# Summing sixteen of the 24 adaLN weight blocks on VectorE, one layer of a hybrid diffusion backbone on Trainium2

## What is computed

```
mod = silu(cond) @ w_ada + b_ada      # cond 2 x 2048, w_ada 2048 x 12288
shift1, scale1, gate1, shift2, scale2, gate2 = split(mod, 6)
h = rms_norm(x) * (1 + scale1) + shift1
m = mixer(h)        # Hyena branch and attention branch, from one projection w_in, gated, then w_out
x = x + gate1 * rms_norm(m)
h = rms_norm(x) * (1 + scale2) + shift2
x = x + gate2 * rms_norm(experts(h))   # 16 SwiGLU experts, each expert takes its own tokens
```

## Time and profile before

| what | value |
|---|---|
| median of three runs | 2590.87 us (2588.39 to 2595.32) |
| the profiled execution's own time | 2595.64 us |
| its span | 2593.7 us (1.94 us of its time lie outside the span) |
| TensorE busy with matmuls | 2409.6 us, 93% |
| VectorE busy | 436.9 us, 17% |
| ScalarE busy | 236.9 us, 9% |
| read from HBM | 640.21 MB, 248 GB/s over the span |
| mean granted TensorE clock | 0.973 of 2.4 GHz |

### The profile page before, as it was taken

One profiled execution on the slowest core, in us unless ns is written; L12 is line 12 of the kernel. 1 busy time (PEld: TensorE's weight loads), 2 busy tenths in 40 slices (PEclk: granted clock), 3 DMA queues, 4 the chain that ended last, 5 costly groups with the idle time before them and its releaser, 6 DMA issues.

```text
span 2593.7 us, 22327 instructions
## 1 busy us (share of the span) xinstructions
PE 2409.6 (93%) x8986; PEld 1132.3 (44%) x8986; DVE 436.9 (17%) x942; ACT 236.9 (9%) x486; POOL 46.0 (2%) x50
## 2 busy tenths in 40 slices
PE   5899999999999999999999997999989887979896
PEld 2355554444466666555554444333322222222222
DVE  4301111323122111000001204001011010101024
ACT  1100001000021111000000002111000000000001
POOL 0000000000000000000000000000000000000000
PEclk8899999999999999999999998999999999999998
DMA  9964454445423122524442223999999999999995
GB/s 362 352 235 167 174 189 155 147 157 198 162 65 98 65 98 76 200 101 159 162 162 99 97 97 136 388 386 415 416 421 422 422 422 422 422 422 421 422 421 209
DMA packets 196650, 644.87 MB, mean 249 GB/s; under 512 B 8423, under 2 KB 57992, under 8 KB 147112
## 3 DMA queue, kind: packets, MB, share of 16 engines
q1 hardware_dynamic: 194312, 635.55, 63.3%
q10 hardware_dynamic: 2208, 8.24, 0.9%
q0 software_dynamic: 64, 0.13, 0.0%
HBM read 640.21 MB, written 3.67 MB: 248 GB/s over the span
## 4 chain that ended last, share of the span: by engine, by line
PE 76%; DMA 19%; DVE 2%; ACT 1%; issue 1%; SPq 1%; DVEq 0%; ACTq 0%; POOL 0%; POOLq 0%
DMA ring<-in_w_up 14%; PE PS L652 13%; PE PS L404 10%; PE PS L419 10%; PE PS L849 8%; PE PS L898 7%; PE PS L687 6%; PE PS L746 6%; PE PS L671 3%; PE PS L378 3%; DMA ring<-in_w_down 2%; DMA ring<-in_w_ada 2%; PE PS L815 1%; PE PS L642 1%; PE PS L790 1%
## 5 line engine op out<-in xcount | busy, mean ns | idle before, releaser
L849 PE MATMUL PS<-ring,RF 128*48 128x512 f32 x1920 | 442.3, 605 | 77.1 <-DMA ring<-in_w_up 75.3
L652 PE MATMUL PS<-RB,ring 128*128 128x384 f32 x1024 | 336.2, 487 | 0.6 <-ACT RE L1047 0.6
L849 PEld LDWEIGHTS PS<-ring,RF 128*48 128x48 f32 x1920 | 132.3, 124 | 372.2 <-issue 371.7
L652 PEld LDWEIGHTS PS<-RB,ring 128*128 128x128 f32 x1024 | 193.9, 190 | 137.9 <-issue 3.4
L404 PE MATMUL PS<-RB,ring 128*128 128x384 f32 x768 | 251.2, 490 | 1.9 <-DMA ring<-in_w_in 1.9
L419 PE MATMUL PS<-ring,RB 128*128 128x512 f32 x576 | 252.4, 593 | 0.0
L898 PE MATMUL PS<-ring,RF 128*48 128x512 f32 x960 | 223.0, 622 | 6.9 <-DVE RF L1700 4.7
L404 PEld LDWEIGHTS PS<-RB,ring 128*128 128x128 f32 x768 | 146.4, 191 | 109.0 <-issue 9.6
L746 PE MATMUL PS<-ring,RC 128*128 128x512 f32 x384 | 169.2, 601 | 5.2 <-DVE RE L1573 4.7
L419 PEld LDWEIGHTS PS<-ring,RB 128*128 128x128 f32 x576 | 108.1, 190 | 132.1 <-issue 131.8
L898 PEld LDWEIGHTS PS<-ring,RF 128*48 128x48 f32 x960 | 64.2, 129 | 161.3 <-issue 149.0
(11 more groups left out here) (241 smaller groups left out, 1313.7 us busy)
## 6 DMA issues: line engine op xcount, KB each, us to landing
ring<-in_w_gate SPq DMA_DIRECT2D x128, 1024.0 KB, 12.3
ring<-in_w_up SPq DMA_DIRECT2D x128, 1024.0 KB, 14.0
ring<-in_w_down SPq DMA_DIRECT2D x128, 1024.0 KB, 13.4
ring<-in_w_ada SPq DMA_DIRECT2D x48, 2048.0 KB, 13.2
ring<-in_w_in SPq DMA_DIRECT2D x40, 2048.0 KB, 8.1
ring<-in_w_attn_o SPq DMA_DIRECT2D x8, 2048.0 KB, 8.3
ring<-in_w_out SPq DMA_DIRECT2D x8, 2048.0 KB, 8.6
ring<-in_w_hy_o SPq DMA_DIRECT2D x4, 2048.0 KB, 8.0
```

The lines of the kernel that those rows point to most:

```text
L652: last = mm(bank(F0, T), wide[:, n % 4, k, t % 2 * P:(t % 2 + 1) * P], hT[:, k, :], start=k == 0, stop=k == KT - 1)
L849: last = mm(bank(n, p0=64 * u, p1=64 * u + SLOTS), xeT[:, kk, 0, :] if first else x_cur[:, kk, :], pieces[:, (2 * i + u) % 8, k * FF + n * ...
```

## The change

Blocks 0 to 7 stay as they are. For blocks 8 to 23:

- VectorE computes, for each of the two vectors c, acc_c[c] = sum over the 16 k-tiles of weights (128x512) times cond (one value per partition): one tensor_scalar and 15 scalar_tensor_tensor for each c, with a drain after each pair (ada_rows). A half block that it has read signals ada_used, a finished block acc_ready.
- TensorE sums the 128 partitions of acc_c into mod columns (ada_sums): eight matmuls a block with 128x128 stationary data and one moving column of ones, where ada and ada_cols had 16 and 4. It waits for acc_ready. The next block on VectorE waits for cols_done, which ada_sums signals.
- Blocks 8 to 13 stay beside the Hyena loop. In QKV only blocks 14 and 15 are left (before: 14 to 19), both late. Blocks 16 to 23 lie beside the attention gates (before: 20 to 23), one for each pair of tiles.
- In the attention gates the order becomes gate, gate, projection, projection, in two pairs of banks (A0, A1), and ada_sums of the block of the pair before stands after the first gate of a pair.
- ScalarE's copies (rows) of these 16 blocks are gone; shift2's and scale2's columns are read after the attention gates.
- The ring's slots are now freed by either engine, so SP waits for blocks_used or ada_used (slot_free).

```diff
+        acc_c = [view(RG, 0, NC_), view(RG, NC_, NC_)]
+        cond = view(SM, 60, KT, 2)
+        one_col = SM[:, 122:123]
+        A0, A1 = (3, 5), (4, 0)
...
-            with sp.Fori(0, 6) as i:
-                turn(i + B_HY, [(w_ada, 0, i + 8), (w_ada, 1, i + 8), (w_in, 0, i + 6), (w_in, 1, i + 6)])
+            turn(B_HY, [(w_ada, 0, 8), (w_ada, 1, 8), (w_in, 0, 6), (w_in, 1, 6)])
+            with sp.Fori(1, 6) as i:
+                for h in range(2):
+                    sp.wait_ge(ada_used, i * 2 + (h - 1))
+                    sp.dma_start(ring[:, h], block(w_ada, h, i + 8)).then_inc(landed[h], 16)
+                for h in range(2):
+                    sp.wait_ge(blocks_used, i * 2 + (4 * B_HY + h - 1))
+                    sp.dma_start(ring[:, 2 + h], block(w_in, h, i + 6)).then_inc(landed[2 + h], 16)
+
+            def slot_free(n):
+                if from_ada(n - 4):
+                    sp.wait_ge(ada_used, by_dve(n - 4))
+                else:
+                    sp.wait_ge(blocks_used, by_pe(n - 4))
...
             for i in range(6):
                 for h in range(2):
-                    half_block(N_QKV + 4 * i + h, w_ada, h, 14 + i)
-                for h in range(2):
-                    half_block(N_QKV + 4 * i + 2 + h, w_in, h, QKV_ORDER[i])
+                    half_block(qkv_at(i) + h, w_in, h, QKV_ORDER[i])
+                if i >= 4:
+                    for h in range(2):
+                        half_block(qkv_at(i) + 2 + h, w_ada, h, 10 + i)
...
-            for c in range(4):
-                for g in range(2):
-                    two_tiles(N_GA + 6 * c + 4 * g, w_in, 12 + c, g)
-                    two_tiles(N_GA + 6 * c + 4 * g + 1, w_attn_o, c, g)
-                    if g == 0:
-                        for h in range(2):
-                            half_block(N_GA + 6 * c + 2 + h, w_ada, h, 20 + c)
+            for p in range(8):
+                two_tiles(N_GA + 4 * p, w_in, 12 + p // 2, p % 2)
+                two_tiles(N_GA + 4 * p + 1, w_attn_o, p // 2, p % 2)
+                for h in range(2):
+                    half_block(N_GA + 4 * p + 2 + h, w_ada, h, 16 + p)
...
+            def ada_sums(b):
+
+                pe.wait_ge(acc_ready, b - 7)
+                for j in range(4):
+                    for c in range(2):
+                        last = mm(PS[:, 6, ds(b * 8 + (2 * j + c), 1)], acc_c[c][:, paired(j)], one_col,
+                                  start=True, stop=True)
                 last.then_inc(cols_done, 1)
...
             with pe.Fori(0, 6) as i:
-                ada(i + B_HY, 0, 7)
                 channels(i)
-                ada_cols(i + 8, 0)
+                ada_sums(i + 8)
...
+                elif p == 32:
+                    ada_sums(14)
...
             for i in range(6):
-                n = N_QKV + 4 * i
-                ada(0, n % 4, 7, n)
-                tokens(n + 2, 0, hT, conv_free if i == 0 else qkv_raw,
+                tokens(qkv_at(i), 0, hT, conv_free if i == 0 else qkv_raw,
...
-                ada_cols(i + 14, 0)
+            ada_sums(15)
...
+            for p in range(KT // 2):
+                n = N_GA + 4 * p
+                for t in (2 * p, 2 * p + 1):
+                    gate(n, KT + t, A0[t % 2], KT + max(0, t - 1))
+                    if p > 0 and t % 2 == 0:
+                        ada_sums(15 + p)
+                block_in(n + 1)
+                for t in (2 * p, 2 * p + 1):
+                    pe.wait_ge(mixed, KT + max(0, t - 1))
...
+                    last.then_inc(blocks_used if t % 2 else proj_tile, 1)
+            ada_sums(23)
...
+            def ada_rows(b, slot, load):
+
+                dve.wait_ge(cols_done, b)
+                for h in range(2):
+                    dve.wait_ge(landed[slot + h], load)
+                    for k in range(HK):
+                        kk, w = h * HK + k, ring[:, slot + h, k, :]
+                        for c in range(2):
+                            if kk == 0:
+                                last = ts_(acc_c[c], w, cond[:, kk, c:c + 1], None, ALU.mult)
+                            else:
+                                last = stt(out=acc_c[c], in0=w, scalar=cond[:, kk, c:c + 1], in1=acc_c[c],
+                                           op0=ALU.mult, op1=ALU.add)
+                        if k == HK - 1:
+                            last.then_inc(ada_used, 1)
+                        if kk < KT - 1:
+                            dve.drain()
+                dve.drain()
+                V.memset(SM[:, 121:122], 0.0).then_inc(acc_ready, 1)
...
             with dve.Fori(0, 5) as i:
+                ada_rows(i + 8, 0, i * 16 + (16 * B_HY + 16))
                 outer_taps(i)
             gated_input(0)
+            ada_load(13, N_QKV - 4)
             outer_taps(5)
...
             qk_norm(2, 9)
+            ada_load(14, qkv_at(4) + 2)
             qk_norm(3, 12)
-
-            read_mods(32, 80, 20)
-            gains(amp[:, 1], SCALE2, C_GPRE2, 1.0)
+            ada_load(15, qkv_at(5) + 2)
+
+            read_mods(32, 64, 16)
...
             for t in range(KT, 2 * KT):
+                if t % 2 == 0:
+                    p = (t - KT) // 2
+                    ada_load(16 + p, N_GA + 4 * p + 2)
                 merge(t)
 
-            read_mods(80, 96, 24)
+            read_mods(64, 96, 24)
+            gains(amp[:, 1], SCALE2, C_GPRE2, 1.0)
```

More of the change, by code:

```diff
@@ L250, in build, with from_ada, by_pe, by_dve @@
         N_QKV = 4 * (B_HY + 6)
-        N_GH = N_QKV + 24
+        N_GH = N_QKV + 16
         N_GA = N_GH + 12
-        N_WO = N_GA + 24
+        N_WO = N_GA + 32
         N_EX = N_WO + 8
+        def from_ada(n):
+            if n < 4 * B_HY or n >= N_WO or N_GH <= n < N_GA:
+                return False
+            if n < N_QKV:
+                return n % 4 < 2
+            return n % 4 >= 2 and n >= N_QKV + 8
+        def by_pe(n):
+            return sum(not from_ada(i) for i in range(n + 1))
+        def by_dve(n):
+            return sum(from_ada(i) for i in range(n + 1))
+        def qkv_at(i):
+            return N_QKV + 2 * i + 2 * max(0, i - 4)
         QKV_ORDER = (4, 5, 0, 1, 2, 3)
@@ L366, in _, with ada @@
             mm, trp = nc.tensor.matmul, nc.tensor.transpose
-            def ada(b, j0, rows_bank, n=None):
+            def ada(b, j0, rows_bank):
                 for h in range(2):
[L372 to L375, removed]
+                    pe.wait_ge(landed[j0 + h], b * 16 + 16)
                     for k in range(HK):
@@ L380, in ada, with ada_cols @@
                     last.then_inc(blocks_used, 1)
-            def ada_cols(c, which, n=None):
-                pe.wait_ge(rows_copied, (c if n is None else n) + 1)
+            def ada_cols(c, which, n):
+                pe.wait_ge(rows_copied, n + 1)
                 src = rowbuf if which == 0 else tmp
@@ L387, in ada_cols @@
                     last = mm(PS[:, 6, ds(c * 8 + 2 * j, 2)],
-                              src[:, j * P:(j + 1) * P] if n is not None else src[:, paired(j)], sel2,
-                              start=True, stop=True)
+                              src[:, j * P:(j + 1) * P], sel2, start=True, stop=True)
+                last.then_inc(cols_done, 1)
+            def ada_sums(b):
[4 more added lines that the diff above has]
+                                  start=True, stop=True)
                 last.then_inc(cols_done, 1)
@@ L662, in _ @@
                 scores(t)
-                gate(n + j // 2, t)
+                gate(n + j // 2, t, read=t)
                 probabilities(t)
@@ L677, in _ @@
             pe.wait_ge(at_oc, NH)
[L678 to L684, removed]
-                pe.wait_ge(mixed, KT + t)
-                for k in range(NH):
-                    last = mm(bank(F1, T), wide[:, pa % 4, k, j % 2 * P:(j % 2 + 1) * P],
-                              qN[k // 4][:, k % 4, :, :].rearrange("p m d -> p (m d)"),
-                              start=k == 0, stop=k == NH - 1)
-                last.then_inc(blocks_used if j % 2 else proj_tile, 1)
-                if j == 3:
-                    ada_cols(20 + t // 4, 0)
+            for p in range(KT // 2):
[7 more added lines that the diff above has]
+                    pe.wait_ge(mixed, KT + max(0, t - 1))
+                    for k in range(NH):
+                        last = mm(bank(A1[t % 2], T), wide[:, (n + 1) % 4, k, t % 2 * P:(t % 2 + 1) * P],
+                                  qN[k // 4][:, k % 4, :, :].rearrange("p m d -> p (m d)"),
+                                  start=k == 0, stop=k == NH - 1)
+                    last.then_inc(blocks_used if t % 2 else proj_tile, 1)
+            ada_sums(23)
             pe.wait_ge(mixed, 2 * KT)
@@ L963, in _ @@
             with act.Fori(0, 6) as i:
-                act.wait_ge(cols_done, i + 8)
-                rows(i * 4 + (4 * B_HY + 2), 7, rowbuf)
                 for j in range(4):
@@ L999, in _ @@
             for i in range(6):
```

(6 more changed lines are left out.)

41 lines of the change are left out of this document (21 added, 20 removed).

## The result

The changed kernel takes 2553.86 us, the median of four runs (2553.50 to 2554.33), against 2590.52 us of the kernel before, run beside it (four runs, 2588.39 to 2595.32). The ratio is 0.9859, with a 95% interval of 0.9848 to 0.9871. The forecast was 2553 us, with a range of 2544 to 2564.

A forecast was written before the change was run, and what follows sets the result against it. The prediction took TensorE to bound the kernel up to the experts and memory from there. It summed -66.9 + 26.6 + 2.4 + 0.6 - 0.5 = -37.8 us against the 2590.87 us median, giving 2553 us, range 2544 to 2564.

The forecast's parts named there:

- What bounds the kernel: TensorE bounds everything up to the experts; the experts stream at memory's rate, starting with TensorE's progress, their length unchanged.
- What is removed and added, by stage: On TensorE, 15 ada and 16 ada_cols go, 66.9 us; 16 ada_sums come, 26.6 us.
- ada_sums: TensorE's small matmuls per block: 16 records at 0.104 us, 1.66 us a block, 26.6 us in all.
- A block's products: VectorE's time for one block: 23.3 us, bounds 21.5 and 25.4.
- The wait for block 15: At the end of QKV, TensorE waits 2.4 us for block 15's products, bounds 0.6 to 4.5.
- Rival A: The clock falls at block 15's wait at the end of QKV: +2.9 us, 2556 us; chance 0.20.
- The clock at channels(0): Without block 8's matmuls ahead, TensorE is idle longer before channels(0): +0.6 us, bounds 0 to 1.5.
- the order in pairs: In the attention gates, the gate, gate, projection, projection order costs TensorE nothing.
- The Hyena loop: VectorE needs 30 us of a 43.1 us turn; w_in lands at 31, wanted at 43, so nothing waits.
- Rival C: Products outlast a turn: Hyena loop bound above 36 us a block, gain gone at 40, 2669 us at 45; chance 0.04.
- Rivals B and D: B: late load at Hyena gates, up to +5 us, 0.13. D: experts' stream not started by TensorE, 2591 us, 0.03.
- records of 0.2 us: Sign of being wrong: ada_sums records on TensorE taking 0.2 us each, then 26 us of the gain gone.

The follow-up runs named there:

- sums_twice: Changed kernel with every ada_sums done twice over, 16 x 16 records more on TensorE; 2603.46 us, ratio 1.0042 to the kernel before.
- one_more: Changed kernel with one more scalar_tensor_tensor of 128x512 on VectorE in each of a block's 16 steps; 2591.38 us, ratio 1.0003 to the kernel before.
- sum14_early: Changed kernel with block 14 summed two parts earlier (p = 30 instead of 32); 2550.16 us, ratio 0.9840 to the kernel before.
- fill_short: Changed kernel with three dense matmuls of 128x512 into an unused bank ahead of ada_sums(15); 2553.77 us, ratio 0.9852 to the kernel before.
- before_pairs: Kernel before with only the attention gates' order in pairs and banks changed, all adaLN blocks still on TensorE; 2591.95 us, ratio 0.9997.
- few_products: Changed kernel without 12 of the 16 product steps of blocks 8 to 23, loads kept; 2551.50 us, ratio 0.9851 to the kernel before.
- two_more: Changed kernel with two more products on VectorE in each of a block's 16 steps; 2677.52 us, ratio 1.0335 to the kernel before.
- early_swap: Changed kernel with block 14 summed earlier and w_in's first half issued ahead of w_ada's second half in the Hyena loop; 2549.13 us, ratio 0.9835.

## Why the prediction was right, and where it was not

- **What bounds the kernel:** right. Stages and chain are TensorE's up to the experts, and the experts moved along with a length of their own. sums_twice shows it.
- **What is removed and added, by stage.** By the prediction's own terms: Hyena -15.8 us (six ada, six ada_cols, six ada_sums, the clock), measured -16.1; QKV -17.1, measured -16.3; attention gates -4.8, measured -4.5. The sum is -37.7 against -36.8 in these stages, and -36.7 between the medians.
- **ada_sums:** forecast 1.66 us, measured 1.77, that is 0.11 us a record where ada_cols had 0.104. The nearest row was a good guide; over 16 blocks it missed 1.8 us.
- **A block's products:** forecast 23.3 us, measured 23.4. The Trainium skill's rule of a flush after every operation ("VectorE: DVE Perf Modes", Terms), which goes with the upper bound of 25.4 us, does not hold here: two operations of 0.74 us without a drain between them take 1.41 us together (one_more's timeline of VectorE), so the second starts 0.67 us after the first. The Trainium skill's 58 + N cycles ("VectorE: DVE Perf Modes", TRN2 errata), an estimate of 594 ns for 512 columns, are too low for these products, which took 748 ns.
- **The wait for block 15:** forecast 2.4 us, measured 2.46 and the only one on acc_ready in these stages. sum14_early takes it away.
- **The clock at that wait:** the sum had no term for it, and that was wrong. Rival A happened, with 0.20, at 1.8 us instead of 2.9. fill_short and sum14_early show that it takes the wait. The argument against it was that half of the stretch is work; in sums_twice the clock fell behind 3.65 us of such work with no wait at all.
- **The clock at channels(0):** +0.6 us forecast; 43.72 instead of 43.47 us, +0.25.
- **What was costed at nothing:** the order in pairs (before_pairs) and contention (few_products) are nothing indeed. The Hyena loop was hidden too, but its slack was misjudged: I set w_in's landing at 8 us after its issue, the median of the earlier trace rows, while it lands 12.6 us after it behind a w_ada load. And I looked for the bound in VectorE's time, when it lay in the queue.
- **Rival C:** its price at 45 us a block was near (2669 us, two_more 2678), by 46 us instead of 54 in the Hyena loop and 46 instead of 40 in the attention gates. Its threshold was wrong. It names 36 us for the loop and places the loss of all the gain at 40; one_more is as slow as before at 34. With the loads in the other order 34 us bind nothing in the loop; 36 itself was not tried.
- **Rivals B and D** did not happen: no wait at the first Hyena output tile, and the experts moved.
- **Slips** that move neither the forecast nor its range: rival B's price of 5 us makes 2558 us, not 2557; at 38.5 us a block rival C's own terms make 32 us, not 29; records of 0.2 us would cost 25 us of the gain, not 26; and memory gives 352 to 362 GB/s in the first two slices of the earlier trace rows, outside the 65 to 235 named.

The total was within 1 us of the forecast by some luck. The clock behind block 15 and the small sums cost 1.8 us each that the sum did not have, and channels(0) 0.35 less than it had: 3.3 us. Yet the three stages came out only 0.9 us short. Most of the 2.4 us that came back can be found in the traces. Channels takes 41.39 instead of 41.48 us in each of the five later turns. In QKV an ada_cols and an ada took 4.49 us together where the sum had 4.40, and the first 16 records of tokens behind them 7.13 instead of 7.03 us. And before, the first scores waited 0.33 us for ScalarE. channels(0) also starts 1.9 us earlier in the profile of the changed kernel, but early_swap has it at 133.77 us, as before, so no run shows that the change does this.

## What to carry to other kernels

When work moves to another engine, its time there is hidden only if the slots that it holds are freed in time too. In one_more a load that waited for the slow consumer held up the next load of the fast one in the same queue (15 us of the Hyena loop), so ask for each moved consumer what stands behind its next load. Bound small operations by the nearest row of the same stationary shape, and judge a change of some us by the lengths of stages in the profiles, as the totals carry the noise of the longest memory-bound stage.

## What the runs showed of the hardware

- Behind sixteen records of one moving column in 1.77 us the granted clock stayed at 1.00 in the loops. Behind thirty-two of them in 3.65 us, without any gap, it fell in 10 of 16 places, at a cost of 1.7 us or more each (12.12 instead of 10.43 us for a gate tile).
- Behind a wait of 2.46 us together with sixteen such records it fell to 0.50, and cost 1.8 us. Behind 2.7 us of dense matmuls and the same records it stayed at 1.00.
- A load of 2 MB landed 12.6 us after its issue when another of the same size had been issued just ahead of it, and 7.8 us after it when it was alone (both in the Hyena loop of the changed kernel).
- VectorE's float32 products with two inputs in SBUF take 748 ns for 512 columns (743 to 754), 0.67 us from start to start without a drain. Block 16's do so too, from 1004 to 1012 us of the changed kernel, where the DMA share is 1.01 to 1.11 and TensorE is busy throughout. Its tensor_scalar of the same size takes 482 ns (32 of them, 478 to 490).
- With 12 of 16 parts of VectorE's 370 us taken away, the Hyena loop, the Hyena gates and the attention gates are as long as before within a tenth of a us (261.20, 310.50 and 347.38 us against 261.14, 310.52 and 347.37).
